# One input projection in three fp32r passes over split operands, its weights streamed in eight parts, late modulation in quarters

## What is computed

```python
sx1, cx1, gx1, sx2, cx2, gx2 = silu(c) @ w_mod + b_mod      # six rows of 1024; c_ctx gives its own
h = rmsnorm(x, norm1) * (1 + cx1) + sx1                     # latent; the context likewise
u, q, k, v, g, r = split(h @ w_in)                          # widths 512, 256, 256, 512, 512, 32
lg = log_sigmoid(r @ w_gk2 + b_gk) / 16                     # forward and backward decays
o = gated linear attention(q, k, v, lg)                     # chunked, state over the chunks
y = concat(pool_mixer(u), rmsnorm(o) * silu(g)) @ w_out
x = x + gx1 * y
x = x + gx2 * moe(rmsnorm(x, norm2) * (1 + cx2) + sx2)      # 16 experts, top 2
out = rmsnorm(x, norm_f)
```

## Time and profile before

| | |
|---|---|
| median of 3 runs | 1023.66 us (1022.66 to 1024.78) |
| the profiled execution | 1024.93 us |
| its span, first to last instruction | 1023.1 us |
| PE busy | 938.6 us, 92% |
| DVE busy | 598.8 us, 59% |
| ACT busy | 355.2 us, 35% |
| mean granted TensorE clock | 0.949 |
| first projection to state loop | 41.4 to 273.8 us |
| state loop | 273.8 to 348.3 us |
| attention to experts | 348.3 to about 561 us |

### The profile page before, as it was taken

The page is one execution under the profiler, slowest core; times in us unless marked ns, Lnnn a source line. Parts: engine busy times, 40 slices in busy tenths (PEclk is TensorE's granted clock), DMA queues, the critical chain, the costliest instruction groups (busy, mean ns, idle before and its releaser), DMA issues. The chain is left out here.

```text
span 1023.1 us, 13258 instructions
## 1 busy us (share of the span) xinstructions
PE 938.6 (92%) x4591; PEld 642.6 (63%) x4592; DVE 598.8 (59%) x804; ACT 355.2 (35%) x476; POOL 190.5 (19%) x212
## 2 busy tenths in 40 slices
PE   4899999999999999999955899999999999999960
PEld 1554544445444445656534788898888988888850
DVE  0246666889433335444438575949967456599933
ACT  1333423100011221212123154637745335477613
POOL 5101000000000010011000132323432233243322
PEclk9699999999999999999975899999999999999985
DMA  9923442420200522111183766979998686699928
GB/s 330 395 82 102 147 165 95 152 82 1 83 0 1 211 116 105 42 42 62 62 300 111 288 206 183 334 241 320 380 362 273 184 305 221 185 339 371 320 40 349
DMA packets 76506, 194.11 MB, mean 190 GB/s; under 512 B 3493, under 2 KB 3626, under 8 KB 76474
## 3 DMA queue, kind: packets, MB, share of 16 engines
q1 hardware_dynamic: 64192, 152.05, 40.9%
q0 software_dynamic: 7680, 25.35, 10.2%
q10 hardware_dynamic: 4602, 16.30, 4.0%
HBM read 167.98 MB, written 25.71 MB: 189 GB/s over the span
## 5 line engine op out<-in xcount | busy, mean ns | idle before, releaser
L1325 PE MATMUL ps<-arena 128*128 128x512 f32 x288 | 128.8, 601 | 0.0
L1333 PE MATMUL ps<-arena 128*128 128x512 f32 (+1 forms) x288 | 119.1, 571 | 0.0
L1464 PE MATMUL ps<-arena 128*128 128x512 f32 x256 | 113.3, 595 | 0.0
L1540 PE MATMUL ps<-w3h,xTh 128*128 128x256 f32 x368 | 105.9, 288 | 0.0
L1540 PE MATMUL ps<-w3h,xTl 128*128 128x256 f32 x368 | 104.1, 283 | 0.0
L1540 PE MATMUL ps<-w3l,xTh 128*128 128x256 f32 x368 | 104.1, 283 | 0.0
L1333 PEld LDWEIGHTS ps<-arena 128*128 128x128 f32 x288 | 54.0, 190 | 64.3 <-issue 62.7
L1325 PEld LDWEIGHTS ps<-arena 128*128 128x128 f32 x288 | 54.2, 193 | 62.5 <-issue 62.5
L1187 DVE TENSOR_TENSOR w1l<-raw,w1h 128x2048 fp32r<-128x2048 f32 x30 | 68.6, 2287 | 29.8 <-ACT w1h L730 29.7
L1464 PEld LDWEIGHTS ps<-arena 128*128 128x128 f32 x256 | 47.4, 190 | 54.4 <-issue 53.6
L730 ACT ACTIVATE w1h<-raw 128x2048 fp32r (+1 forms) x32 | 61.1, 1912 | 58.0 <-PE ps L1540 46.2
(11 more groups left out here) (244 smaller groups left out, 1496.5 us busy)
## 6 DMA issues: line engine op xcount, KB each, us to landing
raw<-in_w_dram SPq DMA_DIRECT2D x48, 2048.0 KB, 12.9
arena<-in_w_mod_dram SPq DMA_DIRECT2D x12, 2048.0 KB, 8.0
arena<-in_w_in_dram SPq DMA_DIRECT2D x4, 2048.0 KB, 15.2
x_rows<-arena ACTq DMA_DIRECT2D x9, 512.0 KB, 2.6
hx_rows<-arena ACTq DMA_DIRECT2D x9, 512.0 KB, 2.6
arena<-in_x_dram SPq DMA_DIRECT2D x8, 512.0 KB, 14.5
arena<-in_w_out_dram SPq DMA_DIRECT2D x2, 2048.0 KB, 9.3
arena<-in_x_dram ACTq DMA_DIRECT2D x8, 512.0 KB, 10.5
```

Source lines behind the costliest of these rows:

```text
L1325: ins = pe.matmul(ps[:, bank, :], hxT[:, k, g[1] * P:(g[1] + 1) * P], w[:, k, :], start=(k == 0), stop=(k == KC - 1))
L1333: ins = pe.matmul(ps[:, bank, 0:m * P], w[:, k, col:col + P], hxT[:, k, t0 * P:(t0 + m) * P], start=(k == 0), stop=(k == KC - 1))
L1464: ins = pe.matmul(ps[:, 5 + h, :], m, w[:, k, :], start=(k == 0), stop=(k == KC - 1))
L1540: ins = pe.matmul(out_ap, parts[l][:, lhs], w_parts[w][:, cols], start=start and n == 0, stop=stop and n == 2)
```

## The change

The scaled rows go to `hx_full` in fp32; ACT copies each tile to `hx_h` rounded to fp32r (`hx_high`), DVE writes the rest to `hx_l` in the same place that the fp32 rows had (`hx_low`). w_in comes in eight `parts` of 256 columns (v, v, u, u, k, q, g, g; 1 MB each) into two raw places. Each part is split in two pieces of 128 x 1024 by ACT (`part_high`, into the one buffer `high`) and DVE (`part_low`, into two buffers by turns). `piece_free` says when a piece of `high` may be overwritten: after the groups of the part before that read it. A product is then three fp32r MATMULs. v and g groups are halved to 256 columns, so there are 54 steps: v at 0 to 9 and 10 to 19, u at 20 to 27, k at 28 to 33 (the two with 256 context tokens first), q at 34 to 37, g at 38 to 45, and the second half of g (46 to 53) in the state loop. `rank_rows` takes both parts of the rows in fp32. The decays start at step 10 (`LAG_L`) and their sums at step 13 (`LAG_C`); `logits` uses banks 2 and 3, ACT takes the absolute value, and `min_and_abs` is gone. The eight late blocks of w_mod come in quarters of 512 KB (two rows of 512 columns a partition) through two places, and `QUARTERS` gives the step of each. The pool mixer's sums start at step 31, three pieces a step up to 37 and one from 38, and end ahead of the state loop, where before the last of them could run. norm2 is multiplied into a2b in one operation at the attention's first step. The experts' code is the same.

```diff
-LAG_L, LAG_C = 4, 6
+LAG_L, LAG_C = 10, 13
...
+HC = HALF // 2
+QUARTERS = ([10 + q for q in range(10)] + [20 + q // 2 for q in range(16)] + [28 + q for q in range(6)])
...
-        groups = ([("v", t) for t in range(NT)] + [("u", p, g) for p in range(NG) for g in range(2)]
-                  + [("k", a, g) for g in range(3) for a in range(2)] + [("q", a, g) for g in range(2) for a in range(2)]
-                  + [("g", t) for t in range(NX)])
+        groups = ([("v", h, t) for h in range(2) for t in range(NT)] + [("u", p, g) for p in range(NG) for g in range(2)]
+                  + [("k", a, 2) for a in range(2)] + [("k", a, g) for a in range(2) for g in range(2)]
+                  + [("q", a, g) for a in range(2) for g in range(2)] + [("g", h, t) for h in range(2) for t in range(NX)])
+        NV = 2 * NT
...
+        parts = [("v", COL_V), ("v", COL_V + HC), ("u", COL_U), ("u", COL_U + HC), ("k", COL_Q + QK), ("q", COL_Q),
+                 ("g", COL_G), ("g", COL_G + HC)]
...
+        def piece_free(m, i):
+
+            if by_rows(m) and by_rows(m - 1):
+                return (S["half_used"], m // 4 + 1) if i == 0 else (S["proj_done"], part_end[m - 1])
+            if by_rows(m) or by_rows(m - 1):
+                return S["proj_done"], part_end[m - 1]
+            return S["proj_done"], block_end(m - 1, i)
...
+        pieces_at = {}
+        for m in range(1, len(parts)):
+            for i in range(2):
+                last = part_end[m - 1] if by_rows(m) or by_rows(m - 1) else block_end(m - 1, i)
+                pieces_at.setdefault(last - 1, []).append((m, i))
...
+        late_turn_at = {QUARTERS[4 * i + 3] + 1: i for i in range(8)}
...
+            def load_part(m):
+                if m >= 2:
+                    sp.wait_ge(S["proj_done"], part_end[m - 2])
+                col = parts[m][1]
+                sp.dma_start(raw_part[m % 2].rearrange("p (k n) -> p k n", k=KC), win_v[:, :, col:col + HC]).then_inc(part_loaded[m % 2], 16)
...
+            for q in range(len(QUARTERS)):
+                for m in range(2, 6):
+                    if q == {2: 2, 3: 12, 4: 19, 5: 27}[m]:
+                        load_part(m)
+                load_late(q)
+            load_part(6)
+            load_part(7)
...
+            def hx_high(t):
+                act.wait_ge(S["hx_a"], t + 1)
+                act.wait_ge(S["hx_v"], t + 1)
+                act.activation(hx_h[:, t], hx_full[t], ACT.Copy).then_inc(S["hx_high"], 1)
+
+            def part_high(m, i):
+                act.wait_ge(part_loaded[m % 2], 16 * (m // 2 + 1))
+                if m >= 1:
+                    act.wait_ge(*piece_free(m, i))
+                act.activation(piece(high_part[:, :], m, i), piece(raw_part[m % 2], m, i), ACT.Copy).then_inc(S["part_high"], 1)
...
+                if t >= 4:
+                    act.wait_ge(S["cum_done"], t - 3)
+                act.activation(spl[:, t % 4, :], ps[:, 2 + t % 2, :], ACT.Abs).then_inc(S["lg_abs"], 1)
+                act.wait_ge(S["lg_abs"], t + 1)
+                act.activation(spl[:, t % 4, :], spl[:, t % 4, :], ACT.Exp, scale=-1.0).then_inc(S["lg_exp"], 1)
                 act.wait_ge(S["lg_exp"], t + 1)
-                act.activation(absl[:, t % 2, :], absl[:, t % 2, :], ACT.Ln, bias=1.0).then_inc(S["lg_ln"], 1)
+                act.activation(spl[:, t % 4, :], spl[:, t % 4, :], ACT.Ln, bias=1.0).then_inc(S["lg_ln"], 1)
 
...
+            for n in range(group_no[("g", 1, 0)]):
+                if n + 2 < NT:
+                    hx_out(n + 2)
+                if n >= 1:
+                    evacuate(n - 1)
+                if n + 2 < NT:
+                    hx_high(n + 2)
+                if n + 4 < NT:
+                    square(n + 4)
                 if 0 <= n - LAG_C - 1 < NT:
                     decay_exp(n - LAG_C - 1)
                 if 0 <= n - LAG_L - 1 < NT:
                     decays(n - LAG_L - 1)
+                for m, i in pieces_at.get(n, ()):
+                    part_high(m, i)
...
+            def hx_low(t):
+                dve.wait_ge(S["hx_high"], t + 1)
+                dve.tensor_tensor(hx_l[:, t], hx_full[t], hx_h[:, t].bitcast(F32), ALU.subtract).then_inc(S["hx_low"], 1)
+
+            def part_low(m, i):
+                dve.wait_ge(S["part_high"], 2 * m + i + 1)
+                dve.tensor_tensor(piece(low_part[m % 2][:, :], m, i), piece(raw_part[m % 2], m, i),
+                                  piece(high_part[:, :], m, i).bitcast(F32), ALU.subtract).then_inc(S["part_split"], 1)
...
+            def late_sum(q):
+                i, part = q // 4, q % 4
+                dve.wait_ge(late_loaded[q % 2], 16 * (q // 2 + 1))
+                if part == 0 and i >= 1:
+                    dve.wait_ge(S["mrow_done"], i)
+                for j in range(2):
+                    k = 2 * part + j
+                    w = late_in[:, q % 2, j, :]
...
+                    link(dve, mc, ins)
+                dve.sem_inc(S["late_used"], 1)
+                if part == 3:
+                    dve.sem_inc(S["macc_ready"], 1)
...
+                dve.scalar_tensor_tensor(out=spl[:, t % 4, :], in0=ps[:, 2 + t % 2, :], scalar=0.0, in1=spl[:, t % 4, :],
+                                         op0=ALU.min, op1=ALU.subtract).then_inc(S["sp_ready"], 1)
 
...
+                dve.wait_ge(S["pool_w_loaded"], 48)
+                dve.wait_ge(S["proj_done"], group_no[("k", 1, 2)] + 1)
...
+                    if at_step == n:
+                        late_sum(q)
+                if n >= pool_from:
+                    for _ in range(3 if n < group_no[("g", 0, 0)] else 1):
                         next(pooling, None)
...
+                for m, i in pieces_at.get(n, ()):
+                    part_low(m, i)
+            for _ in pooling:
+                pass
+            dve.wait_ge(S["mrow_stored"], 16 * 8)
...
+                    for part in range(2):
+                        for c in range(count):
+                            ins = pe.matmul(ps[RANK2 * c:RANK2 * (c + 1), 6, 0:P], w_r[:, k, :],
+                                            hx[part][:, first + c, k, :].bitcast(F32), start=(k == 0 and part == 0),
+                                            stop=(k == KC - 1 and part == 1))
...
+                elif n >= NV:
+                    pe.wait_ge(S["sp_ready"], n - NV + 7)
+                w = [p_[:, :].rearrange("p (k n) -> p k n", k=KC) for p_ in (high_part, low_part[m % 2])]
+                if g[0] == "v" and g[1] == 0:
+                    pe.wait_ge(S["hx_low"], g[2] + 1)
...
+                    c, (t0, count) = g[1] % 2, tok_groups[g[2]]
+                    pe.wait_ge(S["part_split"], 2 * m + c + 1)
+                    out_ap = ps[:, bank_of(n), 0:count * P]
+                for k in range(KC):
+                    if by_rows(m) and n == part_first[m] and k % 4 == 0:
+                        pe.wait_ge(S["part_split"], 2 * m + k // 4 + 1)
+                    for i, (x_, w_) in enumerate(((0, 0), (0, 1), (1, 0))):
+                        if by_rows(m):
+                            ins = pe.matmul(out_ap, hx[x_][:, t, k, :], w[w_][:, k, :],
+                                            start=(k == 0 and i == 0), stop=(k == KC - 1 and i == 2))
+                        else:
+                            ins = pe.matmul(out_ap, w[w_][:, k, c * P:(c + 1) * P], hx[x_][:, t0:t0 + count, k, :],
+                                            start=(k == 0 and i == 0), stop=(k == KC - 1 and i == 2))
+                    if k == 3 and n + 1 == part_end[m] and m in (0, 6):
+                        ins.then_inc(S["half_used"], 1)
                 ins.then_inc(S["proj_done"], 1)
 
             def logits(t):
...
-                    pe.wait_ge(S["lg_min"], 2 * t)
-                pe.matmul(ps[:, 4, :], rT[:, t * P:(t + 1) * P], w_gk[:, :, :].rearrange("p d n -> p (d n)"),
+                if t >= 2:
+                    pe.wait_ge(S["sp_ready"], t - 1)
+                pe.matmul(ps[:, 2 + t % 2, :], rT[:, t * P:(t + 1) * P], w_gk[:, :, :].rearrange("p d n -> p (d n)"),
                           start=True, stop=True).then_inc(S["lg_done"], 1)
...
-            for n in range(group_no[("g", 0)]):
-                if n + 1 < NT:
-                    turn_rows(n + 1)
+            turn_rows(1)
+            for n in range(group_no[("g", 1, 0)]):
+                if n in late_turn_at:
+                    late_turn(late_turn_at[n])
                 proj(n)
+                if n + 2 < NT:
+                    turn_rows(n + 2)
                 if n in R_STEPS:
                     rank_rows(n)
+                if 0 <= n - LAG_L < NT:
+                    logits(n - LAG_L)
                 if 0 <= n - LAG_C < NT:
                     cumulate(n - LAG_C)
```

356 lines of the change are left out of this document (165 added, 191 removed).

## The result

| | before | after |
|---|---|---|
| median of four runs | 1024.22 us | 1044.95 us |
| lowest to highest | 1022.66 to 1025.04 us | 1043.72 to 1046.44 us |
| span of the profiled execution | 1023.1 us | 1044.2 us |
| scores (the end of the state loop) start at | 348.27 us | 367.60 us |
| from there to the span's end | 674.8 us | 676.6 us |

The changed kernel is slower: ratio 1.0205, 95% interval 1.0184 to 1.0226. Forecast were 1018.5 us and a range from 1008 to 1030.

A forecast was written before the change was run, and what follows sets the result against it. It took PE, busy 92% of the span, as the bound: PE's list 36 us shorter, but waits for ACT, DVE and quarters leave 5.2 us, so 1018.5 us against the 1023.66 median; range 1008 to 1030.

The forecast's parts named there:

- PE's list: Whole changed stage: projection groups save 42 us, doubled rank_rows adds 5.6, so PE's own list gets 36 us shorter.
- the Trainium skill's rule: Full 128-row weight loads don't overlap with MATMULs; the prediction instead took the trace's 115 to 120 ns spacing, loads hidden.
- PE alone: Rival, whole changed stage: no wait at all on PE, 989 us; chance 0.04.
- Start to step 10: First half of v: first product at 42.1 us, 4.2 to 4.3 a step, step 10 starts at 94.5.
- ACT or DVE longer in v: Rival, v steps: semaphores add 0.5 us a step over 20 steps, 10 us, giving 1028; chance 0.15.
- Steps 10 to 19: Second half of v: 48.5 us of PE work, 3.9 of softplus waits, 6.5 more at step 19.
- Steps 20 to 30: u and first k steps: 51 us to step 27, then 13.8, late-turn waits included; step 31 starts at 220.9.
- The rival with late quarters: Rival, steps 20 to 27: 512 KB loads take nearer 7.9 us, PE waits 22 more, 1040; chance 0.13.
- Steps 31 to 37: Last k and q steps: DVE's list of 51 us against PE's 38.5, so PE waits 12.5; step 38 at 271.9.
- First half of g: Steps 38 to 45: 23.3 us plus 2.0 for the lower clock, ending at 297.2.
- state loop: Second half of g: 4.5 us a step instead of 8.48, 45.9 in all; scores start at 343.1.
- Behind it: From the scores to the end: no change counted; 1.3 us if the norm2 product lacks cover.

The follow-up runs named there:

- the run of five edits: Changed kernel with evacuation before hx_out, first u part's low split later, two pooling pieces a step, w_in parts on ACT's queue, softplus first: 1005.22 us.
- section 1: Changed kernel with ACT and DVE evacuating group n-1 ahead of hx_out(n+2): 1031.12 us, ratio 1.0065 to the kernel before.
- section 7: Changed kernel with w_in parts 2 to 7 issued on ACT's queue instead of SP's: 1037.08 us, ratio 1.0131 to the kernel before.
- section 5: Changed kernel with two pieces of pooling a step from step 31 to 45, instead of three, then one: 1037.42 us, ratio 1.0124 to the kernel before.
- section 9: Changed kernel with evacuation first, later u split, two pooling pieces, parts on ACT's queue: 1006.29 us; with softplus first too: 1005.22 us.

## Why the prediction was wrong

It forecast 1018.5 and faster; measured 1044.95 and slower. In the profile the scores start at 367.6 instead of 343.1, 24.5 us late: 13.3 of them at step 10, 2.8 in steps 10 to 19, 7.6 in steps 20 to 30, and 0.7 behind. By the prediction's steps:

- **PE's list, 36 us shorter.** Held. 256 columns follow each other in 0.12, 512 in 0.23, and the loads of the weights stay hidden. With most waits gone (the run of five edits) the page counts PE busy for 901.1 us, 37.5 less than before. The sentence that takes the trace over the Trainium skill's rule was right. PE alone was never the question.
- **Start to step 10: the step that failed.** "So a step takes 4.2 to 4.3." I compared ACT's list (4.1) with PE's (3.85) as if they ran freely beside each other. In the order that the code has, product n waits for the evacuation of product n - 2, which stands behind an `hx_out` whose transposes PE issues only behind product n - 1: through two banks the three engines form a chain, 5.8 us long at full clock, 7.3 with the low clock behind the wait. Measured 67.5 us from the first product to step 10 instead of 52.4. With the evacuation first it was 52.3: the sum of the lists was right, and that they can overlap in the order as written was wrong. The rival "ACT or DVE longer in v" pointed to this place with 10 us, but by another mechanism (lengths and semaphores), which section 1 refutes. Before the change the transposes stood ahead of the product, so the same order cost nothing; moving them was part of the change, and I hadn't asked what it did. This step alone doesn't account for all: without it (section 1) the time is 1031.12, still slower than before and just outside the range.
- **Steps 10 to 19.** Three waits of 1.3 (measured 1.21) and step 19 with 11.4 (11.7): held; the stage took 61.7 for 58.9, mostly since a product there takes 3.07 from start to start of what follows for the 2.9 taken, and one ran at a lower clock (4.25, 139.24 to 143.49).
- **Steps 20 to 30.** 75.1 (169.56 to 244.69) instead of 67.5. The late turns waited 3.1, 0.9 and 2.8 for 2.0, 0.7 and 1.5: the place (SP behind parts 4 and 5) was right, as section 7 shows, the term 2.6 us too small. Quarters land in 3.7 by the median for the 3.5 taken, but quarter 19, behind a part, took 6.35. The other 5.0 are mostly the clock, 0.93 in this stretch, which stands in no term: behind the step-19 wait alone the first u product took 7.2 instead of 5.7. I had counted the clock only ahead of g. By the fit of the Trainium skill, "DMA: Bandwidth & Descriptors", section Anatomy of one DMA — SWDGE (gpsimd) path, 2.0 us and 436 KB a microsecond, made for transfers that GpSimd issues, a quarter would be 3.2 as an estimate; the trace, with SP issuing, says 3.7. The rival with late quarters (5.8 us each) is not what happened.
- **Steps 31 to 37.** DVE's list of 51: held, 51.1 (244.69 to 295.75), DVE busy 49.1 of 51.7 us, PE waiting 10.0 (3.3 + 6.7) for the 12.5 taken. The late turn at step 34, its 1 us and the 3.3 that it waits, I had not listed; it costs nothing while DVE ends the stage. The wait ahead of g, which I had put down to pooling, is 2.6 of handover and 4.0 of pooling (section 5).
- **First half of g** 24.5 for 25.3, **state loop** 47.3 for 45.9, 4.47 a step for 4.5: held.
- **Behind it** I counted nothing; 1.8 us more were measured. From the first scores to the end of the pool mixer's first eight MATMULs (L1518) it takes 8.0 us (367.60 to 375.64, at the lower clock until 374), before the change 6.6. In the run of section 1 the scores ran at the full clock there, but PE then waited 2.8 for ACT and the same work took 9.4. So the clock isn't the whole of it; the cause stays open.

The rest of the answer is in section 9: the three passes do pay, 36 us of list and 19 us of time, once the five edits are made. (None of them was tried on the kernel before; there PE waits for only 3.9 us from 40 to 275 us.) The change as it stands gives all of it back in waits and in the lower clock behind them.

## What to carry to other kernels

A step's time is not the longest of the engines' lists but the longest cycle through them: before adding up lists, walk one buffer's cycle (who frees it, behind what that instruction stands, and who issues what that one waits for). Halving a product halves the time in which its bank's evacuation must come round, and work moved from ahead of the product to behind it can close a cycle, so a rotation that was deep enough may not be any more. And put the instruction that frees something ahead of the one that waits, a load that waits for another thing on a queue of its own, and spread filler work over the stages by each stage's room.

## What the runs showed of the hardware

- Waits of 1.8 to 3.1 us on PE were enough for the granted clock to fall, but not each time: of the five products behind such waits the same program had four at the low level in one execution and two in the next, and another with the same first half of v had none. The Trainium skill, "TensorE: Matmul & The Clock Gate", section A second HAM failure mode: psum-queue depth-cycling, describes such swings for short idle stretches between groups; these traces agree.
- A wait can cost more than it lasts: when 10.5 us of them went, the first half of v got 15.2 us shorter, against an execution with four products at the low level; against one with none it is 9.3.
- A product of 128 by 128 in fp32 takes 0.22 us (24 MATMULs for twelve, 2.59 us from their start to the next product's), about twice the 0.12 us that an fp32r one of 256 columns takes.
- A quarter of 512 KB issued 0.4 us behind a part of 1 MB on the same queue was there 6.35 us after its issue, against 3.7 us in the median of all 32.
